# Sparse attention: two gate tiles projected while the index masks are made, and the other ten spread by halves over sixteen heads

## The reference

```python
h = x @ w_in
q, k, v, z, qi, ki, wi = split(h)          # q, z: 2048 wide; k, v: 128; qi: 512; ki: 64; wi: 8
score = sum_h relu(qi_h . ki) * wi_h        # 512 x 512, causal
idx = top_k(score, 128)                     # for each query
logits = q_h . k[idx] * scale               # 16 heads, one k and v for all
probs = softmax(where(valid, logits, -inf))
o = probs @ v[idx]
y = (o * silu(z)) @ w_out
```

## Time and profile before

| | us |
|---|---|
| median of three runs | 1604.64 (1604.2 to 1606.51) |
| the profiled execution, its own time | 1607.34 |
| its span, by the trace | 1605.6 |
| PE busy | 1509.8 (94% of the span) |
| DVE, ACT, POOL busy | 676.8, 527.6, 549.9 |
| PE idle between tile 19 with two products after it and the first masks | 11.07 |
| head loop, from the first transposes to the first product of `w_out` (736.10 to 903.27) | 167.17 |

### The profile page before, as it was taken

One profiled execution on the slowest core, in us unless ns is written; L12 is line 12 of the kernel. 1 busy time (PEld: TensorE's weight loads), 2 busy tenths in 40 slices (PEclk: granted clock), 3 DMA queues, 4 the chain that ended last, 5 costly groups with the idle time before them and its releaser, 6 DMA issues. The chain is left out here.

```text
span 1605.6 us, 23500 instructions
## 1 busy us (share of the span) xinstructions
PE 1509.8 (94%) x9997; PEld 1312.3 (82%) x9997; DVE 676.8 (42%) x1356; ACT 527.6 (33%) x862; POOL 549.9 (34%) x216
## 2 busy tenths in 40 slices
PE   7999999999999999998999899999999997768998
PEld 7898885998997977776887899789889875648897
DVE  6032540232145273695555214541252135688424
ACT  3444225333123223333444212343342244421211
POOL 6323420333332238732643233224342412312121
PEclk9999999999999999998999999999999998978999
DMA  5223220133412322230110431244322200020111
GB/s 162 83 75 94 90 65 15 54 97 131 152 54 79 113 82 89 69 103 27 53 53 27 147 103 57 89 130 113 105 85 73 93 13 1 0 79 1 57 50 53
DMA packets 113750, 121.21 MB, mean 75 GB/s; under 512 B 12529, under 2 KB 107613, under 8 KB 113390
## 3 DMA queue, kind: packets, MB, share of 16 engines
q1 hardware_dynamic: 110096, 113.77, 22.4%
q10 hardware_dynamic: 3550, 5.94, 1.0%
HBM read 113.41 MB, written 6.29 MB: 75 GB/s over the span
## 5 line engine op out<-in xcount | busy, mean ns | idle before, releaser
L193 POOL TENSOR_TENSOR w_low<-w_ring,w_high 128x2048 fp32r<-128x2048 f32 (+1 forms) x91 | 414.2, 4552 | 799.4 <-ACT w_high L184 798.9
L209 PE MATMUL ps<-w_high,xT_high 128*128 128x256 f32 (+1 forms) x1056 | 305.2, 289 | 9.1 <-POOL w_low L451 4.2
L209 PE MATMUL ps<-w_low,xT_high 128*128 128x256 f32 (+1 forms) x1056 | 299.7, 284 | 0.0
L209 PE MATMUL ps<-w_high,xT_low 128*128 128x256 f32 (+1 forms) x1056 | 299.5, 284 | 0.0
L184 ACT ACTIVATE w_high<-w_ring 128x2048 fp32r<-128x2048 f32 (+1 forms) x91 | 171.4, 1884 | 312.1 <-PE ps L209 307.6
L209 PE MATMUL ps<-xT_high,w_high 128*128 128x512 f32 (+1 forms) x600 | 241.3, 402 | 4.0 <-POOL w_low L193 3.0
L209 PE MATMUL ps<-xT_high,w_low 128*128 128x512 f32 (+1 forms) x600 | 238.5, 398 | 0.0
L209 PE MATMUL ps<-xT_low,w_high 128*128 128x512 f32 (+1 forms) x600 | 237.5, 396 | 0.0
L209 PEld LDWEIGHTS ps<-w_high,xT_high 128*128 128x128 f32 x1056 | 203.0, 192 | 16.0 <-issue 6.3
L209 PEld LDWEIGHTS ps<-w_low,xT_high 128*128 128x128 f32 x1056 | 202.9, 192 | 1.7 <-issue 1.7
L209 PEld LDWEIGHTS ps<-w_high,xT_low 128*128 128x128 f32 x1056 | 202.9, 192 | 0.0
(11 more groups left out here) (504 smaller groups left out, 2286.5 us busy)
## 6 DMA issues: line engine op xcount, KB each, us to landing
w_ring<-in_gla_w_in_dram SPq DMA_DIRECT2D x24, 1024.0 KB, 5.3
w_ring<-in_dsa_w_in_dram SPq DMA_DIRECT2D x19, 1024.0 KB, 5.1
w_ring<-in_w_in_dram SPq DMA_DIRECT2D x18, 1024.0 KB, 5.2
w_ring<-in_gla_w_out_dram SPq DMA_DIRECT2D x8, 1024.0 KB, 5.0
w_ring<-in_ple_gate_w_dram SPq DMA_DIRECT2D x8, 1024.0 KB, 5.2
w_ring<-in_dsa_w_out_dram SPq DMA_DIRECT2D x8, 1024.0 KB, 5.1
x_scratch<-x SPq DMA_DIRECT2D x4, 1024.0 KB, 7.0
w_ring<-in_w_out_dram SPq DMA_DIRECT2D x4, 768.0 KB, 4.8
```

Source lines behind the costliest of these rows:

```text
L193: self.nc.gpsimd.tensor_tensor(self.slot(self.w_low, i % RING, k, cols), self.slot(self.w_ring, n % RING, k, cols), self.slot(self.w_high, ...
L209: return self.nc.tensor.matmul(out, lhs, rhs, start=first, stop=last, skip_group_check=not check)
```

## The change

`n_early` grows from 20 to 22: tiles 20 and 21 are projected on PE after tile 19, ahead of `logits(0)`. ACT takes their Tanh (and splits the next chunk) ahead of `exps(0)`; DVE multiplies them after `mask(0)` and `mask(1)`. The ten tiles 22 to 31 make 20 halves for 16 heads: heads 0 to 3 have both halves of a tile (22 to 25), at the two places as before, and heads 4 to 15 one half each, at the second place (between the seven transposes and `logits`). So a tile of 26 to 31 is spread over two heads, and ACT, DVE and POOL deal with it in the second of them.

```diff
-        n_early = DSA_HEADS + n_silu
+        n_early = DSA_HEADS + n_silu + 2
+        late_halves = [(n_early + i // 2, i % 2) for i in range(2 * (n_tiles - n_early))]
+        two_each = len(late_halves) - DSA_HEADS
+        first_half = lambda h: 2 * min(h, two_each) + max(h - two_each, 0)
+        halves_of = lambda h: late_halves[first_half(h):first_half(h + 1)]
+        half_tiles = (range(0, KD // 2), range(KD // 2, KD))
+        late_done = lambda h: [n for n, half in halves_of(h) if half == 1]
...
                     turn_prob(h, 1)
-                    if n_early + h < n_tiles:
-                        project(n_early + h, range(0, KD // 2))
+                    for n, half in halves_of(h)[:-1]:
+                        project(n, half_tiles[half])
                     if h:
                         turn_out(h - 1)
                     turn_prob(h, 2)
                     turn_prob(h, 3)
-                    if n_early + h < n_tiles:
-                        project(n_early + h, range(KD // 2, KD))
+                    for n, half in halves_of(h)[-1:]:
+                        project(n, half_tiles[half])
...
-                    if n_early + h < n_tiles:
-                        project(n_early + h)
+                    for n in late_done(h):
+                        project(n)
...
                 mask(1)
+                for n in range(DSA_HEADS + n_silu, n_early):
+                    project(n)
                 for h in range(DSA_HEADS):
```

## The result

The changed kernel takes 1598.51 us (median of 7 runs) where the kernel before, run beside it, takes 1606.05: a ratio of 0.9950 with a 95% interval of 0.9937 to 0.9964, 8.0 us of 1606. Its profiled execution took 1598.51 us, with a span of 1596.8 against 1605.6. The forecast was 8.4 us less, 1596.2 us, from a median of before that was 1.4 us lower than in these runs; so 1598.51 lies inside the range but 0.5 us above the band that the forecast had by itself (1594.5 to 1598), while the difference is met.

A forecast was written before the change was run, and what follows sets the result against it. DVE's top-k was taken to bound the mask stretch, PE the heads with a tile. Start 0 and heads 8.5 us less, rounded down to 8.4, gave 1604.64 - 8.4 = 1596.2 us; range 1593.5 to 1601.5.

The forecast's parts named there:

- the band that the forecast had by itself: Whole kernel: 8 to 9 us less, 1596.2 us, by itself 1594.5 to 1598; chance 0.70.
- The tiles in the gap: PE's idle 11.07 us before DVE's first mask: two tiles take 11.2 us, first mask 729.48 against 729.40, 0.08 us lost.
- The start of the loop: From the masks to tile 22: DVE's multiply decides, ACT has nearly 2 us to spare; 0.1 earlier to 1.5 later, taken 0.
- The heads: Loop over heads: 11.31 for head 0, 11.74 for 1 to 3, 9.62 for 4 to 13; sum 158.6, 8.5 us less.
- heads of 10.0 to 10.4: Rival on half heads: they pay more than head 12's opening as ACT or DVE fall behind; 1600 to 1604; chance 0.11.
- of 8.9: Rival on half heads: the opening's wait shrinks as DVE runs ahead, 0.7 less each, ten times; 1589; chance 0.04.
- The cross-check: Heads: 11.2 us of PE's work left the loop, 2.7 come back; losing a 2.8 us half wins a head 2.1.
- The end: Last split on POOL and `low(15)`: done 6.9 us into the next phase, 4.6 us to spare; next phase starts about 894.8.
- Beside the masks: POOL's split beside the masks of heads 0 and 1: costs DVE nothing; rival, DVE is held, 1601.7 us, chance 0.06.
- The other side: Rival: a half head is bound by `turn_prob`, copy, `logits`, mask, not PE, and lasts 11.74; 1617 us; chance 0.05.
- the tiles not fitting: Rival at the gap: chunk or bank is not ready, so the tiles delay `logits(0)`; 1604 us; chance 0.04.

The follow-up runs named there:

- the gap filled: The kernel before, with the 48 products of tiles 20 and 21 computed once more ahead of `logits(0)` and not used: 1605.83 us, ratio 0.9982.
- Silu for six: The changed kernel, with tiles 20 and 21 gated whole by ACT's Silu and no multiply on DVE: 1596.26 us, ratio 0.9936.
- Quarters: The changed kernel, with the one half of heads 4 to 15 cut in two quarters, one at each place: 1589.26 us, ratio 0.9887.
- half first: The changed kernel, with the one half of heads 4 to 15 at the first place instead of the second: 1597.19 us, ratio 0.9943.

## Why the prediction was right

- **The tiles in the gap.** 48 products were to end at 729.06 and the first mask to come at 729.48, 0.08 us late. Counted from tile 19's Silu the mask came 0.20 us later than before (11.54 instead of 11.34). A small miss: the first product's way to DVE was 0.54 us (729.32 to 729.86), not the 0.42 of head 11.
- **The start of the loop.** DVE's multiply decided, as forecast, not ACT's split and table load: PE waited 1.34 us for it. Tile 22 starts 18.47 us after the Silu, before tile 20 started 18.29 after it; I took 0. The first transposes themselves came 1.40 us earlier than before, and head 0, counted from them, did not keep its 11.31 us but took 12.91: the two nearly cancel. That the multiplies gave back what the clock had won is shown by two runs: the gap filled (-1.43) and Silu for six (-1.61).
- **The heads.** 9.62 us per head with one half, put together from head 12's opening and head 11's second part; measured 9.61. Heads 14 and 15 took 7.23 and 8.59 (forecast 7.2 and 8.7). This also excludes heads of 10.0 to 10.4 and of 8.9. The cross-check, 11.2 us out and 2.7 back, gave only half of the reason: heads 4 to 11 give back more (they take 76.92 us instead of 93.87, 5.5 less than the 22.4 of products that left them), and heads 12 to 15 hide some of what came to them (35.06 instead of 26.76, 2.9 less than the 11.2 that came). Quarters win back 8.0, more than the 2.7, since they cover also the waits that heads 12 to 15 had all along, 4.93 us.
- **The end.** `low(15)` 6.9 us into the next phase, measured 6.7; no wait behind it. First product of `w_out` at 894.8; measured 895.09, less 0.26 by which this execution reached tile 19 later.
- **Beside the masks.** A mask inside POOL's split took 0.69 us for 512 columns (732.02), as long as before with no split beside it (733.14, below), and the two multiplies 1.28 together, no longer than two of 0.68 apart from one. The rule of the Trainium skill ("SBUF — State Buffer", Who interferes with whom), by which a DVE instruction with at most one input in SBUF, outside its 2-port performance modes, does not contend with GpSimd, agrees with these rows.

```profile
733.14 0.69 DVE L1615 CUSTOM_DVE_ANT_0 prob<-ps,left 128x512 f32<-128x512 f32 x1 [0.95 <-PE ps L209]
```

- **The other side.** Half heads as long as full ones (1617) was excluded by the first half head; the tiles not fitting, by the absence of a pause.

The distance was 8.44 us shorter in the profiled execution against 8.4 forecast, and 8.0 by the ratio. That the first two agree to 0.04 us is in part luck: the start was 0.2 us late, and a sum rounded down by 0.1 and a head 15 that was 0.1 us short made up for it. What the prediction did not see is that the same gain is to be had by the early tiles alone; its own terms say so (heads 0 to 9 at 11.74, four at 7.2), but they were not put together in that order.

## What to carry to other kernels

When an engine's fixed work is spread more evenly over a loop, the sum of the work does not change; what changes is which waits it covers (here the even spread alone won 0.05 us). Price each place in the iteration by the wait that stands there without it, and put there just as much as covers it: here 1.5 us at either place did what 2.9 us at one could not. Work moved into another engine's long stretch is worth its length, less the waits that open where it stood: here 11.2 us were moved and 8.4 won. That holds as long as it ends with that stretch: a third tile, which ran 5.6 us beyond it, cost 1.8 us.

## What was not expected of the hardware

The same program behind the loop took between 700.2 us (half first, 1593.1 less 892.86) and 702.8 (Silu for six, 1595.5 less 892.68) in ten profiled executions, and the stretch ahead of tile 19's Silu between 716.96 and 718.32. Neither goes with the length of the loop. So two spans can differ by 3 us without a cause in the change, which is a third of its gain. The granted clock goes with it: over the stretch behind the loop its mean is 0.95 in the three executions where that lasts longest (702.7 to 702.8) and 0.96 in the other seven. The runs of the kernel before on the second chip show the same tendency: the three shortest spans (1599.2 to 1600.8) have a mean granted clock of 0.974 or 0.975, the four with the lowest clock (0.967 to 0.969) last 1605.5 to 1608.1. What makes the clock differ is left open.
